# Both chunks' doublings done together, and seven products for the mixers' input projections

## The reference, cut to what matters

```python
for l in range(DEPTH):                                  # DEPTH = 2
    h = rmsnorm(x, norm_g[l])                           # [256, 1024]
    proj = h @ w_in[l]                                  # the input projections
    (a_q, a_ff, a_fb, a_i, a_g, b_q, b_k, b_v, b_g, c_s, c_g, merge) = jnp.split(proj, IN_OFFSETS, axis=-1)
    y_a = hgrn2_mixer(a_q, a_ff, a_fb, a_i, ...) * silu(a_g)
    y_b = retention_mixer(b_q, b_k, b_v, ...) * silu(b_g)
    y_c = rwkv7_mixer(c_s, ...) * silu(c_g)
    gates = sigmoid(merge.reshape(b, t, 3, D_MODEL))
    mixed = gates[:, :, 0] * (y_a @ w_branch_a[l]) + gates[:, :, 1] * (y_b @ w_branch_b[l]) \
          + gates[:, :, 2] * (y_c @ w_branch_c[l])
    x = x + mixed @ w_out[l]
```

## Time and profile before

| what | us |
|---|---|
| median of 3 runs | 3360.77 (3359.3 to 3363.44) |
| the profiled execution's own time | 3365.51 |
| its span, first to last instruction | 3363.7 |
| PE busy | 3119.5 (93%) |
| DVE busy | 1713.8 (51%) |
| ACT busy | 723.0 (21%) |
| POOL busy | 256.2 (8%) |

### The profile page before, as it was taken

One profiled execution on the slowest core, in us unless ns is written; L12 is line 12 of the kernel. 1 busy time (PEld: TensorE's weight loads), 2 busy tenths in 40 slices (PEclk: granted clock), 3 DMA queues, 4 the chain that ended last, 5 costly groups with the idle time before them and its releaser, 6 DMA issues.

```text
span 3363.7 us, 42903 instructions
## 1 busy us (share of the span) xinstructions
PE 3119.5 (93%) x17716; PEld 2599.8 (77%) x17716; DVE 1713.8 (51%) x3539; ACT 723.0 (21%) x1389; POOL 256.2 (8%) x326
## 2 busy tenths in 40 slices
PE   8988998999989988999799999899989989998999
PEld 7877886888876877888688887696849749855794
DVE  3546466465321464655644532475237647646475
ACT  3223333132110232333223210100121011013100
POOL 0202111011000030202002000000000000000000
PEclk9998998999999998999899999999989999997999
DMA  5332332323333422323241433444324434431343
GB/s 214 97 96 91 97 109 85 102 84 117 129 105 137 150 79 77 129 91 106 78 134 35 162 104 116 151 169 175 137 88 158 169 118 140 165 115 75 121 168 125
DMA packets 153746, 403.74 MB, mean 120 GB/s; under 512 B 57520, under 2 KB 106800, under 8 KB 109648
## 3 DMA queue, kind: packets, MB, share of 16 engines
q1 hardware_dynamic: 51376, 367.87, 30.8%
q10 hardware_dynamic: 100608, 28.32, 3.5%
q0 software_dynamic: 1568, 4.79, 0.4%
HBM read 388.37 MB, written 12.59 MB: 119 GB/s over the span
## 4 chain that ended last, share of the span: by engine, by line
PE 80%; DVE 12%; DMA 4%; ACT 2%; issue 1%; POOL 0%; ACTq 0%; DVEq 0%; SPq 0%
PE bank L416 23%; PE bank L1898 16%; PE bank L1916 6%; PE bank L1722 6%; PE bank L433 5%; PE bank L1785 3%; PE bank L815 2%; PE bank L834 2%; PE bank L1325 2%; DMA rw_ex<-xT_scratch 1%; PE bank L1927 1%; DVE rw_ex L652 1%; PE bank L825 1%; DMA xT_scratch<-rw_bm 1%; PE bank L454 1%
## 5 line engine op out<-in xcount | busy, mean ns | idle before, releaser
L416 PE MATMUL bank<-h_features,weight_ring 128*128 128x256 f32 x4256 | 981.6, 387 | 12.2 <-DVE y_features L1242 4.9
L416 PEld LDWEIGHTS bank<-h_features,weight_ring 128*128 128x128 f32 x4256 | 810.0, 193 | 131.6 <-issue 9.2
L433 PE MATMUL bank<-weight_ring,h_features 128*128 128x256 f32 (+2 forms) x896 | 201.9, 376 | 1.9 <-ACT h_features L480 1.0
L433 PEld LDWEIGHTS bank<-weight_ring,h_features 128*128 128x128 f32 x896 | 161.5, 190 | 25.1 <-DVE h_features L508 2.3
L1898 PE MATMUL bank<-h_features,weight_ring 128*128 128x128 f32 x1408 | 171.9, 275 | 5.4 <-DVE h_features L508 5.4
L1898 PEld LDWEIGHTS bank<-h_features,weight_ring 128*128 128x128 f32 x1408 | 164.3, 192 | 6.1 <-DVE h_features L508 6.1
L1967 ACT COPY mem_normed<-bank 128x128 f32<-128x128 f32 x88 | 23.3, 265 | 482.7 <-PE bank L1898 477.0
L1722 PE MATMUL bank<-y_features,weight_ring 128*128 128x256 f32 x512 | 120.2, 383 | 0.0
L1325 PE MATMUL bank<-hg_qs,hg_ks 128*128 128x128 f32 x512 | 76.4, 296 | 40.6 <-DVE hg_qs L1479 37.7
L1722 PEld LDWEIGHTS bank<-y_features,weight_ring 128*128 128x128 f32 x512 | 94.9, 190 | 13.5 <-issue 1.3
L1325 PEld LDWEIGHTS bank<-hg_qs,hg_ks 128*128 128x128 f32 x512 | 68.0, 204 | 47.9 <-DVE hg_qs L1479 43.6
(11 more groups left out here) (521 smaller groups left out, 5353.7 us busy)
## 6 DMA issues: line engine op xcount, KB each, us to landing
weight_ring<-in_w_in SPq DMA_DIRECT2D x146, 1024.0 KB, 4.9
weight_ring<-in_f00w SPq DMA_DIRECT2D x33, 1024.0 KB, 4.8
weight_ring<-in_f01w SPq DMA_DIRECT2D x33, 1024.0 KB, 4.8
weight_ring<-in_f10w SPq DMA_DIRECT2D x33, 1024.0 KB, 4.8
weight_ring<-in_f11w SPq DMA_DIRECT2D x33, 1024.0 KB, 4.8
weight_ring<-in_w_b SPq DMA_DIRECT2D x16, 1024.0 KB, 5.0
weight_ring<-in_w_out SPq DMA_DIRECT2D x16, 1024.0 KB, 4.9
weight_ring<-in_conv_in SPq DMA_DIRECT2D x10, 1024.0 KB, 4.8
```

The lines of the kernel that those rows point to most:

```text
L416: m = e.matmul(bank[:, j, :], w[:, k, j * P:(j + 1) * P], x[:, k, :], start=k == 0, stop=k == kt - 1, skip_group_check=True)
L433: m = e.matmul(bank[:, t * n:(t + 1) * n], x[:, k, t * P:(t + 1) * P], w[:, k, :], start=k == 0, stop=k == kt - 1, skip_group_check=True)
```

## The change

1. `SLOTS` goes from 5 to 4, and two sets of `extras` (each 3 x 512 elements a partition) are added for sums of weights. The norm's diagonal and the rope tables move to storage that they share with the mixers' tiles.
2. All 144 chunks of the mixers go through `seven_pe`: seven products of four matmuls each, with 128x128 weights and 128 columns, into two banks. The sums of weights are made by GpSimd (`seven_pool`, four instructions a chunk), which overwrites one quarter in the ring. The sums of the input are made once a layer by DVE (`inputs_dve`). ACT copies one product and DVE puts the result together by four additions into SBUF. What read the bank before now reads that result.
3. The doublings of both chunks are done together, once for each q and direction (`doublings_pe`): 16 matmuls a group with 64x64 weights and 32 columns, the halves of the rows in turn. The four loads of [128 rows x 4 x 128] become four of [64 rows x 8 x 64], all before step 0.
4. The `ORDER` tables of the weaves are new on all engines.

The diff, cut to its core:

```diff
-SLOTS = 5
+SLOTS = 4
+EXTRAS = 2
@@ ORDER, ("mixers0", "tensor"): one line of eight
-        "H2 R20 H2 R5 H11 R4 H R2 H6 B4 R2 B3 H R B2 R5 H2 R2 B R B R H2 R2 B R4 B2 R4 H2 B R3 H2 R3 B R2 B R2 H2 "
+        "H7 R29 H3 B R3 H2 R5 H4 B2 H5 B4 H7 R6 B2 H9 B6 R2 B5 R B R5 H R2 B2 R2 B R2 H2 R4 B R4 H2 B R2 B2 R B R "
+def inputs_dve(e, g, l):
+    dve = g.cd.dve
+    (x11, x12), (x21, x22) = input_quarters(g)
+    t1, t2, t4 = g.x_sums
...
+    e.tensor_tensor(t1, x12, x11, ALU.subtract).then_inc(*dve.up("t1", l))
...
+    e.tensor_tensor(t2, x22, t1, ALU.subtract).then_inc(*dve.up("t2", l))
...
+    e.tensor_tensor(t4, x21, t2, ALU.subtract).then_inc(*dve.up("t4", l))
+    e.wait_ge(*g.cd.pe.at("codes", l))
+    e.tensor_tensor(x12, x22, x12, ALU.subtract).then_inc(*dve.up("t3", l))
+def seven_pool(e, g, S, *name):
+    (a11, a12), (a21, a22) = chunk_quarters(g.w.take(KT, 256, *name))
+    s1, s2, s4 = g.extra.take(*name)
+    for free in g.extra.free(*name):
+        e.wait_ge(*free)
+    e.wait_ge(*g.w.loaded(*name))
+    e.tensor_tensor(s1, a21, a22, ALU.add).then_inc(*S.pool.up("half sum", *name))
...
+    e.tensor_tensor(a21, a11, a21, ALU.subtract).then_inc(*S.pool.up())
...
+    e.tensor_tensor(s2, s1, a11, ALU.subtract).then_inc(*S.pool.up("whole sum", *name))
...
+    e.tensor_tensor(s4, a12, s2, ALU.subtract).then_inc(*S.pool.up("sums", *name))
+def seven_pe(e, g, S, *name, tokens=False):
...
+    first, last = (g.banks.take(S, *name, i).rearrange("p (i t) -> p i t", i=4) for i in range(2))
+    products = ((first[:, 2, :], a[0][0], x[0][0]), (first[:, 0, :], a[0][1], x[1][0]), (last[:, p4, :], a[1][1], t4),
+                (first[:, 1, :], s2, t2), (last[:, p5, :], s1, t1), (last[:, p3, :], s4, x[1][1]),
+                (last[:, p7, :], s3, t3))
+    for i, (out, weights, inputs) in enumerate(products):
+        if i == 0:
+            for free in g.banks.free(*name, 0):
+                e.wait_ge(*free)
+            e.wait_ge(*g.w.loaded(*name))
+        if i == 2:
+            for free in g.banks.free(*name, 1):
+                e.wait_ge(*free)
+        if i == 3:
+            e.wait_ge(*S.pool.at("sums", *name))
+        left, right = (inputs, weights) if tokens else (weights, inputs)
+        for k in range(KT // 2):
+            m = e.matmul(out, left[:, k, :], right[:, k, :], start=k == 0, stop=k == KT // 2 - 1,
+                         skip_group_check=True)
...
+        if i == 6:
+            g.w.done(S.pe, *name)
+            g.extra.done(S.pe, *name)
+        yield
+def seven_act(e, g, S, out, *name):
+    e.wait_ge(*S.pe.at("first", *name))
+    e.copy(quarters(out)[:, 3, :], g.banks.get(*name, 0)[:, 2 * P:3 * P]).then_inc(*S.act.up("first", *name))
+def seven_dve(e, g, S, out, *name):
...
+    e.wait_ge(*S.act.at("first", *name))
+    e.tensor_tensor(q[:, 0:2, :], q[:, 3:4, :].to_broadcast([P, 2, P]), first[:, 0:2, :], ALU.add).then_inc(
+        *dve.up("u2", *name))
+    g.banks.empty(dve, *name, 0)
+    e.wait_ge(*S.pe.at(*name))
+    e.tensor_tensor(q[:, 2:4, :], q[:, 1:2, :].to_broadcast([P, 2, P]), last[:, 0:2, :], ALU.add).then_inc(
+        *dve.up("u3", *name))
+    e.tensor_tensor(q[:, 1:3, :], q[:, 2:4, :], last[:, 2:4, :], ALU.add).then_inc(*dve.up("u4", *name))
+    e.tensor_tensor(q[:, 3, :], q[:, 3, :], last[:, 0, :], ALU.add).then_inc(*dve.up("raw", *name))
+    g.banks.empty(dve, *name, 1)
+def doublings_pe(e, g, l, q, d):
...
+    parts = [(i, rows) for i in range(4 * TT) for rows in ROW_HALVES]
+    for lv in RW_LEVELS:
...
+        for i, rows in parts:
+            m = e.matmul(bank[rows, i], R.scored_a[rows, i // 4, i % 4, 0, rows], level_half(R.x, lv, d)[rows, i],
+                         start=True, stop=True, skip_group_check=True)
...
-                for lv in RW_LEVELS:
-                    src, dst = level_half(R.x, lv, d), level_half(R.xT, lv, 1 - d)
-                    for h in range(4):
-                        m = e.matmul(bank[:, h], R.scored_a[:, c, h, 0, :], src[:, h], start=True, stop=True,
-                                     skip_group_check=True)
+                if step == 0:
+                    yield from doublings_pe(e, g, l, q, d)
```

More of the change, by code:

```diff
@@ L101 @@
 NCF = _at
-CM_NAMES = tuple((f"lvl{h}", P) for h in LEVELS) + (("dir0", T), ("dir1", T))
+CM_NAMES = (tuple((f"lvl{h}", P) for h in LEVELS) + (("dir0", T), ("dir1", T)) +
+            tuple((f"half{h}", 64) for h in (16, 32)))
 CM = {}
@@ L137, in constants @@
         mask(f"lvl{h}", (p // (2 * h) == c // (2 * h)) & (p // h != c // h))
+    for h in (16, 32):
+        r, k = p % 64, c[:, :64]
+        mask(f"half{h}", (r // (2 * h) == k // (2 * h)) & (r // h != k // h))
     for d, (strict, within) in enumerate(((p < c, p <= c), (p > c, p >= c))):
@@ L324, in free, with __init__, take, done @@
         i = self.index[name]
-        return [self.done_at[self.order[i - SLOTS]]] if i >= SLOTS else []
+        return [self.done_at[self.order[i - SLOTS]]] if i >= SLOTS and self.done_at else []
     def landing(self, *name):
         return self.sems[self.index[name] % SLOTS], 16
+class Extras:
+    def __init__(self, ring):
+        self.ring, self.order, self.index, self.done_at = ring, [], {}, {}
+    def take(self, *name):
+        if name not in self.index:
+            self.index[name] = len(self.order)
+            self.order.append(name)
+        i = self.index[name] % EXTRAS
+        return [self.ring[:, i, s * 512:(s + 1) * 512].rearrange("p (k n) -> p k n", k=KT // 2) for s in range(3)]
+    def done(self, count, *name):
+        self.done_at[name] = count.now()
+    def free(self, *name):
+        i = self.index[name]
+        return [self.done_at[self.order[i - EXTRAS]]] if i >= EXTRAS and self.done_at else []
 class Tiles:
@@ L402, in w_in_load @@
     at, n = g.w_in_at[name]
+    if name != "codes":
+        g.extra.take(name, l)
     load_chunk(e, g, piece(g.t[f"w_in{l}"], at, KT, n), KT, n, name, l)
@@ L579, in shifted_dve, with shifted_raw_act, shifted_raw_dve @@
     g.banks.empty(S.dve, *name)
+def shifted_raw_act(e, g, S, out, raw, tile0, *name):
+    yield
+    e.wait_ge(*S.dve.at("raw", *name))
+    for j in range(2):
+        a = e.activation(out[:, j, :], raw[:, j, :], ACT.Copy, scale=g.mu_rest[:, tile0 + j:tile0 + j + 1])
+    a.then_inc(*S.act.up(*name))
+    yield
+def shifted_raw_dve(e, g, S, out, raw, tile0, l, *name):
+    yield
+    e.wait_ge(*S.act.at(*name))
+    for j in range(2):
+        k, o = tile0 + j, out[:, j, :]
+        e.scalar_tensor_tensor(o[:, 1:T], raw[:, j, 0:T - 1], g.col(f"mu0{l}", k), o[:, 1:T], ALU.mult,
+                               ALU.add).then_inc(*S.dve.up())
+        e.wait_ge(*S.dve.now())
+        v = e.scalar_tensor_tensor(o[:, 0:T - 1], raw[:, j, 1:T], g.col(f"mu1{l}", k), o[:, 0:T - 1], ALU.mult,
+                                   ALU.add)
+    v.then_inc(*S.dve.up(*name))
+    yield
 def codes_act(e, g, l):
@@ L1028, in rwkv_pool @@
     for q in range(4):
+        for name in ("c_r", "c_k", "c_v", "c_g"):
+            yield from seven_pool(e, g, S, f"{name}{q}", l)
         yield
@@ L1527, in hgrn_pool @@
     for q in range(4):
+        for name in ("a_q", "a_ff", "a_fb", "a_i", "a_g"):
+            yield from seven_pool(e, g, S, f"{name}{q}", l)
         for level in HG_SCALES:
@@ L1734, in branch_act, with branch_dve @@
         yield
-        e.wait_ge(*S.pe.at(f"m{br}{s}", l))
         e.wait_ge(*S.dve.at(*(("end", l, 3) if s == 0 else ("merged", l, s - 1))))
-        e.activation(gates, pairs(g.banks.get(f"m{br}{s}", l)), ACT.Sigmoid).then_inc(*S.act.up("gates", l, s))
-        g.banks.empty(S.act, f"m{br}{s}", l)
+        yield from seven_act(e, g, S, gates, f"m{br}{s}", l)
+        e.wait_ge(*S.dve.at("raw", f"m{br}{s}", l))
+        e.activation(gates, gates, ACT.Sigmoid).then_inc(*S.act.up("gates", l, s))
         yield
-def branch_dve(e, g, S, before, l, gates, part, wname, chunks):
+def branch_dve(e, g, S, before, l, br, gates, part, wname, chunks):
     for s in range(4):
         mixed = g.mixT3[:, 2 * s:2 * s + 2, :]
+        yield from seven_dve(e, g, S, gates, f"m{br}{s}", l)
         yield
```

345 lines of the change are left out of this document (208 added, 137 removed), and 108 rows, old and new, of the table ORDER.

## The result

The changed kernel took **3692.39 us** (median of 4 runs, 3683.83 to 3700.07), beside 3360.31 us of the kernel before on the same chip: a ratio of 1.099 [1.095, 1.102], 332 us slower. The forecast was 3286 us, a gain, with a range of 3215 to 3375 us. The rival on the slower side (3407 us) falls short of the measured time too.

What follows compares the result with a forecast made beforehand. The prediction took PE to bound each mixer weave. Its terms, -92.9 - 25 - 10 + 27 + 2 + 8 + 16 = -75 us, took the profiled 3365.5 to 3290.6, or 3286 us from the runs' median; range 3215 to 3375.

Steps and rivals of the forecast that it cites:

- If a third of it meets a DVE addition ... at a loss of 0.42 in 0.84 us, DVE gets 58 us more: In each weave, a third of POOL's 346 us of new work overlaps DVE's two-SBUF-operand additions, adding 58 us to DVE.
- 27 for all of DVE's lateness: PE's 78 us of waits for DVE's chains lengthen with DVE's load: +27 us, bounds 0 and +78.
- 16 for GpSimd's queue: Sums queued behind H's levels on GpSimd delay PE 2 us at each of 8 q stages: +16 us.
- The two engines hinder each other: POOL and DVE additions running together take 0.85 and 0.84 us, where alone they take 0.61 and 0.42.
- It still fits in 950: DVE's load in a weave grows from 487 to some 655 us, +35%, and fits in 950.
- more chunks at the boundary: The new order lays more chunks over the q boundary: lower bound 0 for the +27 us of waits for DVE.
- so 0: Four weight-ring slots for five: loads and sums finish within the 14 us before use, cost 0; 4.3 us of waits could double.
- Seven products, -92.9: Mixer chunks on PE: seven products save 0.645 us in each of 144 chunks, -92.9 us, if PE keeps going.
- The doublings, -25: Joint doublings on PE at 1.9 us a group, 152 us in place of 176.8: -25 us; side by side, -70.
- The loads, -10: Second reload of blocks goes; half of PE's 19.9 us of waits saved: -10 us, bounds 0 and -20.
- GpSimd can't feed PE: Slower rival, 3407 us, chance 0.14: sums late at each chunk's fourth product, +137 us; decides from 6.3 us a chunk upward.
- Banks and t3: Two banks a chunk; the third product waits until the previous chunk is put together: +8 us, bounds 0 and +36.

Runs made afterwards that it cites:

- experiments 1 to 3: Changed kernel with GpSimd's four sums a chunk left out (3456.59 us), replaced by memsets as long (3548.87 us), or by memsets of 8 columns (3450.67 us).
- experiment 8: Changed kernel without GpSimd's sums (3456.6 us), with one of VectorE's four additions a chunk kept and three left out: 3446.97 us.
- Experiment 10: New order, joint doublings and four slots, but eight products and results read from the bank as before, no sums: 3438.07 us, beside 3358.8 in the old order.
- experiment 7: Changed kernel without GpSimd's sums (3456.6 us), with five ring slots; products of sums read the chunk's own quarters: 3445.15 us.

## Why the prediction was wrong

- **"If a third of it meets a DVE addition ... at a loss of 0.42 in 0.84 us, DVE gets 58 us more"** is the first step that failed. The pair in the earlier trace rows was read as two instructions that share evenly, each at half speed. They don't even cover the same time: POOL's runs from 119.64 to 120.49, DVE's from 119.94 to 120.78, so DVE ends 0.29 us after POOL, as the held ones do here. Beside an addition of 1.27 us DVE is held until it ends, and in six cases until several have. DVE's busy time rose by 279 us from no sums to true ones (1904.5 to 2183.6), 140 a weave where the forecast had 58, and experiments 1 to 3 price it: 144 us for what only true additions hold, 92 more for a busy GpSimd, of a total of 236. The sum had 27 for all of DVE's lateness and 16 for GpSimd's queue.
- **"The two engines hinder each other"** was charged only for two SBUF operands. That one-input instructions of DVE are held, by memsets too, was no term. Nor was it counted that the change makes more of DVE's instructions read two SBUF operands.
- **"It still fits in 950"**: the load did fit (735 of 1195). It was the wrong test. PE waits for DVE's chains, which were held (for L757 37.7 us, without sums 8.6), and work taken off elsewhere (experiment 8: 135 us) gave 10.
- **The new order had no term.** The prediction even counted more chunks at the boundary as a gain. Experiment 10 puts it at 79 us with before's work in it; with the copy it is 109. That is the largest piece beside the additions, and the reason why a free GpSimd still leaves the kernel slower than before. Of the 79, some 11 may be the fourth slot (from experiment 7), which "so 0" had called free: weights cost PE 23.0 us, not 4.3. How the rest divides between rows of the order and B's tiles stays open.
- **Seven products, -92.9.** PE's work fell as forecast where nothing else changed (0.64 us a chunk). "If PE keeps going" failed: of 91 us only 51 arrive in the old order and 12 in the new. In the new order the products took 7.69 us a chunk with eight and 7.20 with seven, so 72 us went, and PE then waited 32 us more. The mean clock was 0.921 against 0.930. What each cost isn't priced apart.
- **The doublings, -25.** PE's saving was right by the bound (side by side, -76 alone and -60 in the changed kernel), its effect nothing as long as PE waited for all four loads.
- **The loads, -10**, had the wrong sign: +20 us of waiting. The step "issues four loads for a direction as before" overlooked that they were issued two and two. Now all four stand ahead of the first product.
- **GpSimd can't feed PE**: rejected by its own bound. Sums took 5.6 us a chunk, under the 6.3 from which it decides, and PE waited 25 us for them (16 forecast). The danger was right as to the engine and wrong as to the mechanism. Its 137 us for the queue did not come: the same queue with tiny steps cost nothing.
- **Banks and t3**: not tested by themselves. PE's waits for DVE's additions (L584 and L595) come to some 68 us in the groups of L561 (its first row above shows 22.2 and 5.1 of them), where 8 were forecast. Yet experiment 8, which takes three of the four away where GpSimd is free, gains only 10.
- **What no run tried**: sums made by DVE, or true sums by GpSimd in the old order. Whether seven products can pay in this kernel stays open.

Do short pieces of products cost PE more than long ones? The timeline of the changed kernel seems to say so:

```profile
57.92 1.06 PE L561 MATMUL bank<-mixers_x_sum,weight_ring 128*128 128x128 f32 x8
...
58.81 1.95 PE L561 MATMUL bank<-mixers_x_sum,mixers_extras 128*128 128x128 f32 x16
...
61.49 2.84 PE L561 MATMUL bank<-h_features,weight_ring 128*128 128x128 f32 x24
```

A single product takes 1.06 us, 133 ns an instruction; three in a row 2.84, 118 each; the long stretch of the earlier trace rows 112. But the next piece begins 0.89 us after the single one began (58.81), before it ends, and that is 8 x 112 ns. The rest of a piece's length is its end, which lies under the next. So these rows show no price for standing alone, and adding up the busy times of interleaved groups counts such ends twice.

The rule of the page "GPSIMD Engine Reference" of the Trainium skill, to do two-input additions on VectorE (section 4.1), was the right warning. Its clause on contention (section on specifications) names VectorE instructions with two SBUF inputs and those in a 2-port perf mode. The first kind is borne out here (484 to 1182 ns); whether the held one-input instructions ran in such a mode, no row shows.

## What to carry to other kernels

Before moving work to GpSimd, ask what DVE does at that moment on the chain, not whether GpSimd is fast enough: here 5.6 us of sums a chunk, on an engine that was nearly idle, cost 236 us. Price a rewritten order and a longer way of a result as edits of their own, by running the old instructions in the new order. And when several loads share one semaphore, let the first user wait only for what it reads: that alone turned a change worth nothing into 1.6%.

## What the runs showed of the hardware

- A VectorE instruction with two SBUF inputs, 0.48 us long, waits for the GpSimd addition that is running and ends 0.3 us after it: 29 of 96 took 1.1 to 1.5 us. Six waited for several additions and took 3.5 to 7.7 us.
- A memset of GpSimd held a TENSOR_SCALAR of VectorE with one SBUF input (347 to 1234 ns on average) and not a SCALAR_TENSOR_TENSOR with two (484 and 484). VectorE's additions with an operand in PSUM were not held by GpSimd's additions (at most 423 ns).
- Matmuls of 64x64 weights that alternate between the two halves of the rows run side by side: 32 instructions of 32 columns take 1.12 us (median of 80 groups), and those looked at start in pairs 7 ns apart.
- A wait of PE can cost more than its length: 30 us of waits gone gave 48 in one kernel, 34 gave 62 in another. Of the profiled executions' 41 and 70 us, 13.5 and 49 are PE's busy time, with the mean clock up by 0.005 and 0.014.
